# One product with a square of ones for the RMS sums, and a 128x256 power on GpSimd

## The reference

```
xn  = rmsnorm(x)
h   = xn @ w_in                       # (256, 2048) @ (2048, 13312)
o_a = neighbourhood_attention(q, k, v) * silu(na_z)
o_b = gated_linear_scan(forward) + gated_linear_scan(backward)   # 8 heads of 128 values
o_b = o_b * rsqrt(mean(o_b * o_b, over the 128 values of a head) + 1e-6) * hg_norm_w
o_b = o_b * silu(hg_z)
y   = sigmoid(g_a) * (o_a @ w_branch[:1024]) + sigmoid(g_b) * (o_b @ w_branch[1024:])
out = x + rmsnorm(y @ w_out) * norm_post_w
```

## Time and profile before

| | |
|---|---|
| median of three runs | 861.09 us (859.41 to 861.1) |
| the profiled execution | 860.94 us |
| its span | 859.2 us, granted TensorE clock 0.997 |
| TensorE busy | 841.3 us (98% of the span) |
| VectorE busy | 636.9 us (74%) |
| ScalarE busy | 404.2 us (47%) |
| GpSimd busy | 46.6 us (5%) |

### The profile page before, as it was taken

The page is one execution under the profiler, slowest core; times in us unless marked ns, Lnnn a source line. Parts: engine busy times, 40 slices in busy tenths (PEclk is TensorE's granted clock), DMA queues, the critical chain, the costliest instruction groups (busy, mean ns, idle before and its releaser), DMA issues.

```text
span 859.2 us, 14528 instructions
## 1 busy us (share of the span) xinstructions
PE 841.3 (98%) x4913; PEld 730.7 (85%) x4913; DVE 636.9 (74%) x1304; ACT 404.2 (47%) x667; POOL 46.6 (5%) x51
## 2 busy tenths in 40 slices
PE   6999999999999999999999999999999999999995
PEld 5888888888888888888888888888888888888884
DVE  4877876886888688688878868876875777774444
ACT  6554444435444453644544454345444555554442
POOL 5300000000100000010000001000000000000002
PEclk9999999999999999999999999999999999999998
DMA  9967658565675766666566666656566866576522
GB/s 287 239 183 190 170 148 206 154 191 151 169 191 147 180 180 165 177 164 176 162 167 183 160 181 157 172 164 175 157 186 165 226 185 178 180 275 213 190 100 99
DMA packets 270966, 153.44 MB, mean 179 GB/s; under 512 B 15240, under 2 KB 261088, under 8 KB 270304
## 3 DMA queue, kind: packets, MB, share of 16 engines
q1 hardware_dynamic: 269936, 149.17, 63.5%
q10 hardware_dynamic: 1008, 3.98, 1.2%
HBM read 151.04 MB, written 2.10 MB: 178 GB/s over the span
## 4 chain that ended last, share of the span: by engine, by line
PE 96%; DMA 1%; DVE 1%; ACT 1%; POOL 0%; DVEq 0%; issue 0%; SPq 0%; ACTq 0%
PE psum L960 52%; PE psum L962 26%; PE psum L1034 3%; PE psum L1155 3%; PE psum L1157 3%; PE psum L1156 3%; DMA raw<-in_w_in 1%; PE psum L1020 1%; PE psum L1009 1%; PE psum L989 1%; PE psum L1047 1%; PE psum L1039 0%; PE psum L998 0%; PE psum L1054 0%; ACT w_hi L387 0%; DVE big L922 0%
## 5 line engine op out<-in xcount | busy, mean ns | idle before, releaser
L960 PE MATMUL psum<-act_hl,w_hi 128*128 128x512 f32 x1664 | 593.2, 400 | 0.0
L962 PE MATMUL psum<-act_hl,w_lo 128*128 128x256 f32 x1664 | 463.9, 279 | 0.0
L597 DVE TENSOR_TENSOR w_lo<-raw,w_hi 128x1024 fp32r<-128x1024 f32 x270 | 328.0, 1254 | 75.6 <-ACT w_hi L387 75.1
L960 PEld LDWEIGHTS psum<-act_hl,w_hi 128*128 128x128 f32 x1664 | 312.3, 188 | 73.2 <-DVE w_lo L597 3.1
L962 PEld LDWEIGHTS psum<-act_hl,w_lo 128*128 128x128 f32 x1664 | 313.7, 189 | 0.0
L387 ACT ACTIVATE w_hi<-raw 128x1024 fp32r<-128x1024 f32 x272 | 272.8, 1051 | 30.8 <-PE psum L1157 25.7
L398 ACT ACTIVATE part<-psum 128x256 f32<-128x256 f32 x104 | 39.6, 381 | 261.1 <-PE psum L962 261.1
L960 PE MATMUL psum<-branch_hl,w_hi 128*128 128x512 f32 x256 | 90.7, 399 | 0.0
L962 PE MATMUL psum<-branch_hl,w_lo 128*128 128x256 f32 x256 | 71.9, 281 | 0.0
L960 PEld LDWEIGHTS psum<-branch_hl,w_hi 128*128 128x128 f32 x256 | 48.1, 188 | 12.2 <-DVE branch_hl L763 0.3
L657 DVE TENSOR_TENSOR hg<-hg 128x128 f32<-128x128 f32 x224 | 50.7, 288 | 0.3
(11 more groups left out here) (124 smaller groups left out, 543.3 us busy)
## 6 DMA issues: line engine op xcount, KB each, us to landing
raw<-in_w_in SPq DMA_DIRECT2D x104, 1024.0 KB, 5.7
raw<-in_w_branch SPq DMA_DIRECT2D x16, 1024.0 KB, 6.0
raw<-in_w_out SPq DMA_DIRECT2D x16, 1024.0 KB, 5.1
bias_t<-in_na_rel_bias SPq DMA_DIRECT2D x32, 96.0 KB, 5.7
big<-in_x SPq DMA_DIRECT2D x2, 1024.0 KB, 6.3
big<-in_x ACTq DMA_DIRECT2D x2, 1024.0 KB, 6.8
out<-big SPq DMA_DIRECT2D x5, 256.0 KB, 2.7
wide<-in_norm_post_w ACTq DMA_DIRECT2D x1, 1024.0 KB, 4.7
```

The costliest lines, as they stand in the source:

```text
L597: nc.vector.tensor_tensor(w_lo[:, i, :], raw[:, r, 1024 * h:1024 * (h + 1)], w_hi[:, i, :].bitcast(F32), ALU.subtract).then_inc(lo_ready, 1)
L960: nc.tensor.matmul(sums[h][:, :], w_hi[:, i, w], operand[:, k, :], start=first, stop=False, skip_group_check=True)
L962: ins = nc.tensor.matmul(sums[h][:, 0:T], w_lo[:, i, w], operand[:, k, 0:T], start=False, stop=last, skip_group_check=True)
```

## The change

The sums of squares come from one product: a 128x128 square of ones is the weights and `o_sq` (128x256) is what streams, so that each partition gets every token's sum, 128x256 in PSUM, already features by tokens. VectorE's mean square works on 128x256 and writes `rst_rows` in SBUF. GpSimd takes the power -0.5 of these 128x256 elements in place. The spreads (L743) and the transposes (L1062) with their semaphores are gone, and `hgrn_out` waits for the power and reads `rst_rows`. The level-1 product, which writes over the sums in `ps_lvl[1]`, now waits for the mean square having read them.

```diff
--- before.py
+++ after.py
@@ -146,7 +146,6 @@
         ssum, msq, rstd = small2[:, 40:42], small2[:, 42:44], small2[:, 44:46]
         nmax, rsum, rinv = small2[:, 46:50], small2[:, 50:54], small2[:, 54:58]
         neg_half = small2[:, 58:59]
-        hg_ms, hg_rst = small2[:, 59:61], small2[:, 61:63]
         y_sums = (o_sq, o_h)
         post_w = wide[:, :, :].rearrange("p a b -> p (a b)")
 
@@ -189,8 +188,7 @@
         f_tanh, b_tanh, hz_tanh = sem("f_tanh"), sem("b_tanh"), sem("hz_tanh")
         dec_ready, lvl_done, lvl_taken = sem("dec_ready"), sem("lvl_done"), sem("lvl_taken")
         hg_out, osq_ready, ms_done = sem("hg_out"), sem("osq_ready"), sem("ms_done")
-        ms_ready, rst_ready, rst_spread, rst_turned = (
-            sem("ms_ready"), sem("rst_ready"), sem("rst_spread"), sem("rst_turned"))
+        ms_ready, rst_ready = sem("ms_ready"), sem("rst_ready")
         ob_ready, ob_hi, ob_lo = sem("ob_ready"), sem("ob_hi"), sem("ob_lo")
         hg_step, ob_step = sem("hg_step"), sem("ob_step")
 
@@ -353,7 +351,7 @@
             def power(g):
 
                 pool.wait_ge(ms_ready, g + 1)
-                nc.gpsimd.tensor_tensor(hg_rst, hg_ms, neg_half.to_broadcast([P, 2]), ALU.pow).then_inc(rst_ready, 1)
+                nc.gpsimd.tensor_tensor(rst_rows, rst_rows, neg_half.to_broadcast([P, T]), ALU.pow).then_inc(rst_ready, 1)
 
             mask_bias(0)
             with loop(pool, 1, NG) as g:
@@ -736,13 +734,7 @@
 
             def mean_square(g):
                 dve.wait_ge(ms_done, g + 1)
-                nc.vector.tensor_scalar(hg_ms, ps_lvl[1][:, 0:2], 1.0 / P, EPS, ALU.mult, ALU.add).then_inc(ms_ready, 1)
-
-                dve.wait_ge(rst_ready, g + 1)
-                for i in range(2):
-                    ins = nc.vector.tensor_scalar(rst_rows[:, i * P:(i + 1) * P], ones[:, :], hg_rst[:, i:i + 1], None,
-                                                  ALU.mult)
-                ins.then_inc(rst_spread, 1)
+                nc.vector.tensor_scalar(rst_rows, ps_lvl[1][:, 0:T], 1.0 / P, EPS, ALU.mult, ALU.add).then_inc(ms_ready, 1)
 
             def hgrn_out(g):
 
@@ -750,9 +742,9 @@
                 dve.wait_ge(hz_tanh, g + 1)
                 ob_s.done(nc.vector.scalar_tensor_tensor(out=hth, in0=hth, scalar=1.0, in1=hz, op0=ALU.add,
                                                          op1=ALU.mult))
-                dve.wait_ge(rst_turned, g + 1)
+                dve.wait_ge(rst_ready, g + 1)
                 ob_s.done(nc.vector.scalar_tensor_tensor(out=o_h, in0=o_h, scalar=column(half_hgw, g),
-                                                         in1=ps_lvl[1][:, 0:T],
+                                                         in1=rst_rows,
                                                          op0=ALU.mult, op1=ALU.mult))
                 ob_s.settle(dve)
                 ob_s.end()
@@ -1028,7 +1020,7 @@
                 if level == 0:
                     wait(pe, osq_ready, g)
                 if level == 1:
-                    wait(pe, ob_ready, g)
+                    wait(pe, ms_ready, g)
                 for i in range(2):
                     j = 1 - i if level == LEVELS - 1 else i
                     ins = nc.tensor.matmul(dst[:, i * P:(i + 1) * P], k_dec[:, b, i * P:(i + 1) * P],
@@ -1050,17 +1042,7 @@
 
             def square_sum(g):
                 pe.wait_ge(osq_ready, g + 1)
-                for i in range(2):
-                    ins = nc.tensor.matmul(ps_lvl[1][:, i:i + 1], o_sq[:, i * P:(i + 1) * P], ones[:, 0:1],
-                                           start=True, stop=True)
-                ins.then_inc(ms_done, 1)
-
-            def turn_rst(g):
-                pe.wait_ge(rst_spread, g + 1)
-                for i in range(2):
-                    c = slice(i * P, (i + 1) * P)
-                    ins = nc.tensor.transpose(ps_lvl[1][:, c], rst_rows[:, c], block[:, 0, :])
-                ins.then_inc(rst_turned, 1)
+                nc.tensor.matmul(ps_lvl[1][:, 0:T], ones[:, :], o_sq, start=True, stop=True).then_inc(ms_done, 1)
 
             def attention(g, s):
                 if s == 2:
@@ -1087,8 +1069,6 @@
                     hgrn_sum(g - 1)
                 if s == 6:
                     square_sum(g - 1)
-                if s == 7:
-                    turn_rst(g - 1)
 
             def group(g, first):
                 for s in range(IN_SLOTS):
```

## The result

The changed kernel takes 1150.28 us (median of four runs, 1149.01 to 1150.72) against 860.93 for the kernel before. The ratio is 1.3364, with a 95% interval of 1.3347 to 1.3381: slower by a third. The forecast was 1114, with a range of 862 to 1160.

What follows compares the result with a forecast made beforehand. TensorE, busy 841.3 of 859.2 us, was taken as the bound: 860.94 - 1.8 (queue) + 202.3 (seven loop stops) + 35.3 (eighth stop) + 17.6 (clock) = 1114 us, range 862 to 1160.

Steps and rivals of the forecast that it cites:

- The bound and the two prices: Whole kernel: TensorE is the bound, so an edit costs only through its queue or a wait it stands in.
- The length of the power: GpSimd's power of 128x256, called X: taken as 38.0 us (35 to 43), from one- and two-column times.
- the upper bound: GpSimd's 128x256 power: every further column costs 147 ns, as the second did, giving 38.0 us.
- The second rival: GpSimd's power streams like an addition, below 9.1 us and hidden in the loop; 859.1 us at 1.4; chance 0.20.
- the first (overlap in part): GpSimd's power overlaps its columns in part, lasting 9.1 to 30 us; time 865 to about 1050; chance 0.18.
- X - 9.1: TensorE's stop in each of seven loop groups, for a power of X us; 202.3 us in all at 38.0.
- X - 2.7: TensorE's stop at the eighth step, after the loop, for a power of X us; 35.3 us at 38.0.
- Interference: Beside the power, VectorE's two-input work is held, or the power is held up: 1142 or 1146 us; chance 0.12.
- the prediction's own sign: TensorE's stops: if longer than the power's length less 9.1 us, the prediction is wrong and there is interference.
- The clock: TensorE returns from each of eight stops below full clock, losing 2.2 us each, 17.6 us in all.
- The saving: TensorE's queue over eight steps: one product replaces two sums and two turns, 1.8 us less (0.6 to 1.8).
- The lower bound: TensorE's queue: with every turn worth 0.14 us, eight steps save only 0.6 us.

Runs made afterwards that it cites:

- the run with the multiplication: Changed kernel with GpSimd's power of 128x256 replaced by a multiplication of the same elements: 860.48 us against 859.71, ratio 1.0003.
- the sizes: Kernel before, with added powers of 3, 4, 8, 16, 32 and 64 columns of a scratch buffer that nobody reads: 860.83 us.
- The filled stops: Changed kernel with TensorE multiplying ones with ones in each of the seven loop stops: 1142.93 us with 136 products, 1135.81 with 149.
- the partial powers: Changed kernel with the power taken of only the first 32, 64 or 128 columns: 864.3, 895.0 and 988.8 us.

## Why the prediction was right

- **The bound and the two prices.** TensorE's queue and TensorE's waits explain the whole difference. The span grew by 289.3 us. Of that 271.1 are stops (271.4, less 0.3 that the run with the multiplication has too), about 18.7 are the clock's, and 0.8 go off as saved; the 0.3 left over lie ahead of the first power.
- **The length of the power.** The slope between one and two columns, 147 ns, held up to 256, as the sizes show, at 160 ns. That is why the upper bound was the right one to take. The prediction had two sizes alone, and no row of its own ruled out a loop that takes several columns at once; it gave that 0.18, and only the sizes above settle it. The slope was taken too low by 8%: 38.0 us against 41.2. It is the largest error in the sum: 3.2 us eight times, 25.8 us of the 36 by which the forecast was short. The second rival (it streams like an addition) and the first (overlap in part) are both refuted by the straight line.
- **When it is due.** X - 9.1 in the loop and X - 2.7 after it hold at 64, 128 and 256 columns, the first where no addition follows the power (1.46, 11.66 and 32.06 measured; 1.5, 11.7 and 32.1 by formula), the second as it stands (38.4 measured, 38.5 by formula).
- **Interference.** I gave it as a rival in two forms, VectorE held for the length of the power and the power held by VectorE. Neither happens: the power lasts 41.25 us in the loop and 41.12 after it, where VectorE has nothing to do, and VectorE is held for 0.3 us at the power's start alone. A third form did: the bias addition queues behind the power and so starts just when VectorE takes up L746, in the same 0.2 us. It costs 1.4 us in each of six stops, 8.5 us in all, and 10 in the time. By the prediction's own sign, stops longer than X - 9.1, this term was wrong: it stood at nothing in the sum. The row that shows such a meeting stood ahead of the prediction; what I missed is what is queued behind the power on GpSimd.
- **The clock.** 17.6 us forecast, 2.2 for each of eight stops. From the first power to the eighth the changed kernel takes 780.4 us, the run with the multiplication 529.8: 250.6, less 233.0 of stops, leaves 17.6, or 2.5 for each of seven; that this is the figure forecast for eight is chance. It is also half of the 35.3 us that TensorE worked at half speed. The eighth stop adds 1.1 by the same account of what follows it (39.2 longer, 38.1 of it stop). Behind it half speed lasted 5.9 us and cost 2.6; over the next 90 us 1.6 came back, because a pair of products took 0.347 us where it took 0.353 in the run with the multiplication, and no run shows why. The filled stops show that it is the clock. The forecast's 2.2 us had been read at the start of the kernel before, where the granted clock reads 1.00 (window of 5 to 13 us), as the prediction says; whether it was the clock there no run shows, and the size came out near all the same. Where I failed was in the expectation for the partial powers: I took short stops to be free. The Trainium skill, TensorE: Matmul & The Clock Gate, section HAM oscillation — how this bites in real kernels, tells of a loop that comes back cold after every wait; the trace agrees: TensorE came back at half speed behind each of the seven stops of 32 to 33.5 us in the loop.
- **The saving.** This term was mis-sized the other way: 1.8 us forecast, 0.7 measured from first to eighth power, 0.8 between the two profiled spans, and nothing that can be told from no change in the medians. I had credited the turn with the whole 0.31 us up to the next record, and 0.1 of it stays without the turn. The lower bound, 0.6, was nearer.

The sum with the measured terms: 860.9 - 0.8 + 7 x 33.3 + 38.1 + 18.7 = 1150, for 1150.3. Against the forecast of 1114 that is 25.8 more for the power's length, 8.5 for the addition, 1.1 for the clock and 1.0 for the saving, together some 36.

## What to carry to other kernels

Where an operation has only been seen on a few elements, compare two sizes of it before using another operation's rate: a difference of 147 ns between one and two columns foretold 38 us for 256, and it was 41. This power is paid by the column of 128 partitions: the same 256 sums, laid out with tokens on the partitions, made a power of 0.7 us. A stop of TensorE can cost more than its length (here 2.5 us on average for half clock behind it), and lengthening one instruction also moves whatever is queued behind it into new company.

## What was not expected of the hardware

- GpSimd's power on float32 takes 160 ns a column from 8 to 256 columns, some sixty times the 2.6 ns of its addition, and it takes 41.1 to 41.25 us for 256 columns whether or not VectorE works beside it.
- VectorE's instructions on SBUF operands run at full speed beside GpSimd's power (41.1 us each, eight times, at most 1.4 us of cost), except the one that starts within 0.2 us of the long power, which takes 0.3 us more. They do not beside its addition: L746 went from 0.47 to 1.90 us beside an addition of 1.79 us.
- Stops of TensorE of 2.6 to 3.2 us were followed by the low clock thirteen times out of fourteen, and one of 2.91 us was not; two of 1.5 and 1.7 us were not either. How long half speed then lasted, 3.0 to 6.3 us, did not go by the length of the stop: behind seven stops of 32 to 33.5 us it was 3.0 to 6.2 us.
